# A two-block float32 kernel: the moving streams of the split products run backwards, and ten weight buffers get different starting places

## The reference

```
for l in range(DEPTH):                      # first block; the second has the same order, with other mixers
    x = x + 0.5 * swiglu(rms_norm(x), w_gate[l], w_up[l], w_down[l])     # 1024 -> 2816 -> 1024
    x = x + hybrid_mixer(rms_norm(x), w_in[l], ...)                      # three attentions, gates, output
    x = x + 0.5 * swiglu(rms_norm(x), ...)
...
def swiglu(h, w_gate, w_up, w_down):
    return (silu(h @ w_gate) * (h @ w_up)) @ w_down
```

## Time and profile before

| | |
|---|---|
| median of 2 runs | 2814.77 us (2814.58 to 2814.96) |
| span of the profiled execution | 2812.3 us, 2.5 us less than the median |
| TensorE busy | 2792.6 us, 99% |
| weight loads busy | 2396.6 us, 85% |
| VectorE busy | 1921.3 us, 68% |
| ScalarE busy | 1554.0 us, 55% |
| GpSimd busy | 241.5 us, 9% |
| DMA | 503.82 MB, mean 179 GB/s |

### The profile page before, as it was taken

The page is one execution under the profiler, slowest core; times in us unless marked ns, Lnnn a source line. Parts: engine busy times, 40 slices in busy tenths (PEclk is TensorE's granted clock), DMA queues, the critical chain, the costliest instruction groups (busy, mean ns, idle before and its releaser), DMA issues.

```text
span 2812.3 us, 40293 instructions
## 1 busy us (share of the span) xinstructions
PE 2792.6 (99%) x15556; PEld 2396.6 (85%) x15556; DVE 1921.3 (68%) x3180; ACT 1554.0 (55%) x2718; POOL 241.5 (9%) x187
## 2 busy tenths in 40 slices
PE   9999999999999999999999999999999999999998
PEld 8889888888889888888888987888888888878887
DVE  6756676747655667756568777776566687777765
ACT  6545656545545656545456556455455465655553
POOL 0010011010010011010014100110100141001100
PEclk9999999999999999999999999999999999999999
DMA  6544445555544345555554344555555554445553
GB/s 242 191 171 158 149 156 182 193 185 190 195 167 152 139 172 194 199 190 195 195 193 179 136 163 159 210 194 182 199 189 195 183 187 153 158 156 184 209 185 135
DMA packets 75055, 503.82 MB, mean 179 GB/s; under 512 B 8784, under 2 KB 10480, under 8 KB 19184
## 3 DMA queue, kind: packets, MB, share of 16 engines
q1 hardware_dynamic: 74576, 501.07, 50.2%
q10 hardware_dynamic: 288, 0.17, 0.0%
HBM read 500.12 MB, written 1.08 MB: 178 GB/s over the span
## 4 chain that ended last, share of the span: by engine, by line
PE 93%; DVE 4%; POOL 2%; issue 1%; ACT 1%; DMA 0%; SPq 0%; DVEq 0%; ACTq 0%
PE ps L1544 45%; PE ps L1579 21%; PE ps L1585 11%; PE ps L1563 9%; PE ps L1606 3%; POOL wlo L2498 2%; DVE wlo L2038 1%; PE ps L1701 1%; PE ps L1699 1%; DVE conv L2327 1%; PE ps L1726 1%; PE ps L1716 0%; PE ps L1717 0%; PE ps L1718 0%; DVE ps L2144 0%
## 5 line engine op out<-in xcount | busy, mean ns | idle before, releaser
L1777 ACT ACTIVATE whi<-raw 128x1024 fp32r<-128x1024 f32 (+3 forms) x938 | 977.5, 1045 | 600.3 <-PE ps L1544 426.1
L2038 DVE TENSOR_TENSOR wlo<-raw,whi 128x1024 fp32r<-128x1024 f32 (+2 forms) x894 | 1084.1, 1220 | 219.9 <-ACT whi L1777 218.9
L1579 PE MATMUL ps<-xT_both,whi 128*128 128x512 f32 x2560 | 641.6, 393 | 0.0
L1544 PE MATMUL ps<-whi,xT_both 128*128 128x512 f32 (+2 forms) x2336 | 628.9, 391 | 2.6 <-DVE xT_both L2061 1.6
L1579 PEld LDWEIGHTS ps<-xT_both,whi 128*128 128x128 f32 x2560 | 461.1, 189 | 82.6
L1544 PEld LDWEIGHTS ps<-whi,xT_both 128*128 128x128 f32 x2336 | 425.5, 188 | 83.7 <-issue 9.3
L1585 PEld LDWEIGHTS ps<-xT_both,wlo 128*128 128x128 f32 x2560 | 349.3, 191 | 24.9
L1585 PE MATMUL ps<-xT_both,wlo 128*128 128x256 f32 x2560 | 357.1, 282 | 0.0
L1544 PE MATMUL ps<-wlo,xT_both 128*128 128x512 f32 (+2 forms) x1168 | 354.6, 385 | 0.3 <-DVE wlo L2038 0.3
L2118 DVE TENSOR_TENSOR h<-h,ps 128x256 f32<-128x256 f32 x320 | 127.0, 418 | 203.1 <-ACT h L1826 203.1
L1544 PEld LDWEIGHTS ps<-wlo,xT_both 128*128 128x128 f32 x1168 | 218.4, 188 | 43.7 <-DVE wlo L2038 1.4
(11 more groups left out here) (315 smaller groups left out, 2526.7 us busy)
## 6 DMA issues: line engine op xcount, KB each, us to landing
raw<-in_w SPq DMA_DIRECT2D x435, 1024.0 KB, 4.8
vr<-in_vrows SPq DMA_DIRECT2D x19, 512.0 KB, 5.6
raw<-in_w SPq DMA_DIRECT2D x12, 768.0 KB, 4.3
raw<-in_w SPq DMA_DIRECT2D x10, 896.0 KB, 4.5
sums<-scratch SPq DMA_DIRECT2D x8, 512.0 KB, 4.4
raw<-in_w SPq DMA_DIRECT2D x4, 832.0 KB, 4.4
raw<-in_w SPq DMA_DIRECT2D x4, 576.0 KB, 3.7
raw<-in_w SPq DMA_DIRECT2D x4, 512.0 KB, 6.9
```

The costliest lines, as they stand in the source:

```text
L1544: made = e.matmul(bank[:, 0:c1 - c0], xs[:, kt, sl], ws[:, j * w + c0:j * w + c1], start=kt == 0 and n == 0, stop=kt == job.nk - 1 and n == 2)
L1579: e.matmul(bank[:, :].rearrange("p (n x) -> p n x", n=2), hi[:, o:o + 128], job.xt.both[:, :, kt, :], start=kt == 0, stop=False, skip_grou ...
L1777: e.activation(out, raw, ACT.Copy).then_inc(*mark("hi", i))
L2038: e.tensor_tensor(out, raw, hi.bitcast(F32), sub).then_inc(*mark("lo", i))
```

## The change

It has three parts that belong together, and one that stands apart.

- In `rows` the moving operand (weights) is read from the last address to the first, while the output in PSUM is written forwards. So that the result stays in order, `kernel` packs the columns of these pieces mirrored, in cuts of up to 512 (`backward`).
- In `columns` and `wide` the moving operand (activations) is read backwards, and the output is written backwards too, so every value lands where it did. The weights of these pieces (`STANDING`, and the up products after the first chunk) are packed as before. In the wide form the two blocks keep their order and each is mirrored in itself.
- `dt_rows` and the attention products are left as they are.
- In `memory` fills of 8 float32 (32 bytes) stand before whi1 to whi4 and before each wlo. From the place where whi0 begins, the starts within 256 bytes are 0, 32, 64, 96, 128 for `whi` and 160, 192, 224, 0, 32 for `wlo`. The activations' halves keep the place of `whi0`.

The number and the order of the instructions are the same on every engine.

```diff
+STANDING = ("qk1", "xbc", "qc", "kc", "dt")
+
+
+def backward(key, width):
+    standing = key[3] > 0 if key[1] == "up" else key[0] in STANDING
+    return 0 if standing else min(width, 512)
...
     many("raw", NRAW, [128, BLOCK])
-    many("whi", NHL, [128, PIECE], F32R)
     at_line = nc.sbuf_base % LINE
-    many("wlo", NHL, [128, PIECE], F32R)
+    for name, fills in (("whi", (0, 8, 8, 8, 8)), ("wlo", (8, 8, 8, 8, 8))):
+        m[name] = []
+        for i, n in enumerate(fills):
+            if n:
+                sbuf(f"{name}{i}_fill", [128, n])
+            m[name].append(sbuf(f"{name}{i}", [128, PIECE], F32R))
...
-                    made = e.matmul(bank[:, 0:c1 - c0], xs[:, kt, sl], ws[:, j * w + c0:j * w + c1],
+                    made = e.matmul(bank[:, 0:c1 - c0], xs[:, kt, sl], ws[:, j * w + c0:j * w + c1][:, ::-1],
...
-                    made = e.matmul(out, ws[:, o:o + 128], xs[:, kt, :], start=kt == 0 and n == 0 and c % 2 == 0,
+                    made = e.matmul(out[:, ::-1], ws[:, o:o + 128], xs[:, kt, ::-1], start=kt == 0 and n == 0 and c % 2 == 0,
...
-                e.matmul(bank[:, :].rearrange("p (n x) -> p n x", n=2), hi[:, o:o + 128], job.xt.both[:, :, kt, :],
+                e.matmul(bank[:, :].rearrange("p (n x) -> p n x", n=2)[:, :, ::-1], hi[:, o:o + 128],
+                         job.xt.both[:, :, kt, ::-1],
...
-                made = e.matmul(bank[:, 256:512], lo[:, o:o + 128], job.H[:, kt, :], start=False,
+                made = e.matmul(bank[:, 256:512][:, ::-1], lo[:, o:o + 128], job.H[:, kt, ::-1], start=False,
...
-            _, width, kts = pieces[i]
+            key, width, kts = pieces[i]
+            first, turn = off, backward(key, width)
             for idx, kt, ranges in kts:
                 for name, c0, c1 in ranges:
                     dst[:, off:off + c1 - c0] = a[name][idx][128 * kt:128 * kt + 128, c0:c1]
                     off += c1 - c0
+            if turn:
+                cut = dst[:, first:off].reshape(128, -1, turn)
+                dst[:, first:off] = cut[:, :, ::-1].reshape(128, -1)
```

## The result

The changed kernel takes 2853.0 us (median of 2 runs, 2852.34 to 2853.66), against 2814.8 us: a ratio of 1.0136 with a 95% interval from 1.0106 to 1.0165. It is slower by 38 us: less than the 2% (56 us) that the prediction took for the smallest difference worth calling, but well clear of the interval. The prediction was 2747 us, with a range of 2670 to 2835.

A forecast was written before the change was run, and what follows sets the result against it. TensorE, busy 99%, was taken as the bound. Surcharges falling from 13.7 to 8.3 ns gave 73 us, 93% kept as 68; 2812.3 - 68 = 2744.5, plus 2.5, gives 2747 us, range 2670 to 2835.

The forecast's parts named there:

- the surcharge as the only term: TensorE step time above its columns at 2.4 GHz: 13.7 ns for each of 13,592 products, 186 us, all the change can take from.
- What the surcharge is made of: Moving columns of one product meeting the next one's weight load in SBUF; streams going the same way would meet seldom.
- The size, 8.3 ns in the middle of 3.3 and 13.3: Surcharge forecast for reversed streams on every split product, down from 13.7 ns: 73 us less, 68 kept.
- The 3.3: Surcharge in ns of the first narrow step after the wide ones, read as 110 ns; low end of the middle taken.
- 230 and 240: First two 512-column steps of L1579 after the switch from 256, in ns, read to the view's 10 ns.
- the two 288-column pairs: Pairs of 288-column steps taking 0.26 and 0.27 us, read as surcharges of 10 and 15 ns; used to bound the fills.
- The settled 13.3: Surcharge in ns of the steady 120 ns steps of 256 columns; high end of the middle taken.
- The fills at 0, within 5 ns: Spread weight-buffer starts by themselves, forward streams: priced at 0, bounds -5 and +5 ns a product, 68 us to either side.
- The rival of the lost line: Ten different starts bring every product to unsettled steps, 5 to 8 ns more each: 2883 to 2924 us; chance 0.09.
- PSUM: Rival: downward writes in L1563, L1579 and L1585 cost more, up to 1,055 us at two cycles a column; chance 0.05.
- A fixed cost of a product: Rival: the surcharge is a fixed cost of a float32r product; time 2797 to 2815, say 2806 us; chance 0.34 (2775 to 2825).
- the slower cases: The two rivals that forecast a slower kernel: downward writes into PSUM, 0.05, and the lost common line, 0.09.

## Why the prediction was wrong

- **What bounds the kernel, and the surcharge as the only term**: right. TensorE stayed at 99% and 93% of the chain, the longest named wait didn't grow (3.0 us before, 1.8 after), and the whole difference is in the steps: over the whole trace the mean surcharge went from 14.1 ns (13.7 in the prediction's sum) to 17.2.
- **What the surcharge is made of**: the step that failed. I read the unequal steps as the moving stream and the weight load meeting each other, and expected them to meet less when they run the same way. The load's own hold-up did vanish (192 to 188 ns), but it vanished with forward streams and fills as well, where the time rose by 24 us. The loads cut to 16 columns left the backward 512-column step at 233.6 ns, so the load's length isn't what a backward stream pays for. Forward, the short load made the 512-column step longer. One row argued against my account ahead of the result, and I used it only for the size and against a rival: with 16 columns loaded, the surcharge was still 10.4 ns. Even that figure was one state of two, since the same products have 6.7 ns behind backward rows.
- **The size, 8.3 ns in the middle of 3.3 and 13.3**: wrong in sign for 61% of the products. Streams of 512 columns went to 20, those of 256 to 11.6. I took one price for all lengths; the trace after shows two. The 3.3 was misread as well. It comes from a start rounded to 10 ns, and the trace's own times, which are in ns, have 113 ns for that step, a surcharge of 6.3 (6.6 in the mean of all such steps); the middle would have been 10, and the forecast some 50 us less instead of 68, with the same sign. The "230 and 240" are 233 and 236, and the two 288-column pairs have 12.5 and 16. The steps nearest to the truth for 512 columns were those right after a switch (20 and more), which I had called unsettled. The settled 13.3 was near the best of its form, and no mean over meetings.
- **The fills at 0, within 5 ns**: the size was in the bounds. They cost 24 us alone (4.5 ns on a 512-column product of the rows form and 2.5 on one of the wide form, while the narrow ones gained 1 to 2) and 2 us on backward streams. The rival of the lost line named this mechanism and a price of 68 to 109 us; it was right on the fills' run in kind and too high by a factor of about three or more, and it wasn't what made the changed kernel slow.
- **PSUM**: rightly held unlikely; the wide form downwards has 20.0 ns and the rows form upwards 20.1.
- **A fixed cost of a product**: wrong too, since a uniform distance of 64 bytes gives the narrow half a mean of 7.3 ns.
- **The range**: its upper end stood at 20 us above before, because I gave the slower cases 0.14. All its rows came from forward streams on one common line, and I took their 13.3 ns for a middle where it was near the best of its form.

What stays open is why a stream settles where it does: why the backward one costs about 2.5 ns for 64 columns, and why the forward one has 13.3 with a full load from the same place and more with a short one. So the runs show what costs, the backward 512-column stream by itself and the spread starts, but not the mechanism that sets the step. A weight load that runs in the other direction would tell more, and wasn't tried.

## What to carry to other kernels

Where TensorE is the bound and its float32r products run back to back, the step between starts depends on where the moving and the stationary operand begin within 256 bytes, on the direction of the stream and on the products before, by up to 7 ns in the mean of a form, on steps of 120 to 230. Each shape has its own best setting: turn or move one form at a time and read its step in the timeline, before one rule is applied to all. A regular step in the trace is a state that can be lost, and its regularity is no sign of a fixed cost.

## What the runs showed of the hardware that I had not expected

- A 512-column float32r product of the down product takes 226.4 ns a step forward on the common line, and backward about 233.3 (20.0 ns over 213.3) there, with loads of 128 or 16 columns; at the eight places of the fills the backward surcharge is 20 to 21 ns.
- Less work can be slower by the step: with the load cut from 128 to 16 columns the forward step of 512 columns went from 226.4 to 232.1 ns, while that of 256 columns went from 120.0 to 113.1, and the whole kernel, in one run, took 2816.2 us.
- Moving the activations by 64 bytes against the weights takes the 256-column step from 118.8 to 113.8 ns.
- The step of one form depends on the form before it: the same forward wide half has 16.7 ns after a forward narrow half and 13.5 after a backward one, and the 24 forward products of L1600 take 117.1 ns each behind forward rows and 113.3 behind backward ones.
